# Strassen down projection of a float32 trunk: first sums on POOL, two more units split by ACT and DVE, two ACT steps moved

## The reference

```python
def conv_ffn(x, w_up, conv_w, conv_b, w_down):
    hdn = x @ w_up                                 # 512 x 1024 @ 1024 x 5632
    hdn = causal_dwconv(hdn, conv_w, conv_b)       # 3 taps along the tokens
    val, gate = jnp.split(hdn, [D_FF], axis=-1)    # D_FF = 2816
    return (jax.nn.gelu(gate) * val) @ w_down      # 512 x 2816 @ 2816 x 1024

...
for i in range(DEPTH):                             # DEPTH = 2
    ...
    ff = conv_ffn(x, f_w_up[i], f_conv_w[i], f_conv_b[i], f_w_down[i])
    x = layer_norm(ALPHA * x + ff, ln2_g[i], ln2_b[i])
    gate = jax.nn.sigmoid(x @ ple_gate_w[i] + ple_gate_b[i])
    x = x + gate * (p[i] @ ple_w[i])
```

## Time and profile before

| | before |
|---|---|
| median of three runs | 1246.64 us (1245.94 to 1247.58) |
| profiled execution | 1247.68 us, span 1245.6 us |
| PE busy | 1231.5 us (99%) |
| DVE busy | 731.9 us (59%) |
| ACT busy | 428.2 us (34%) |
| POOL busy | 731.8 us (59%) |
| granted clock, mean | 0.997 |

### The profile page before, as it was taken

The page is one execution under the profiler, slowest core; times in us unless marked ns, Lnnn a source line. Parts: engine busy times, 40 slices in busy tenths (PEclk is TensorE's granted clock), DMA queues, the critical chain, the costliest instruction groups (busy, mean ns, idle before and its releaser), DMA issues.

```text
span 1245.6 us, 17102 instructions
## 1 busy us (share of the span) xinstructions
PE 1231.5 (99%) x5733; PEld 1000.0 (80%) x5733; DVE 731.9 (59%) x1112; ACT 428.2 (34%) x719; POOL 731.8 (59%) x994
## 2 busy tenths in 40 slices
PE   9999999999999999999999999999999999999998
PEld 6887777788888888778788778888888888778787
DVE  6555556565545644898744374374644443898842
ACT  4445444222222123661244484112222222662141
POOL 7554467719877774005677547929887775003673
PEclk9999999999999999999999999999999999999999
DMA  5211132303322232864243212312222233675221
GB/s 198 70 68 68 68 118 89 115 8 111 101 101 97 89 132 70 262 197 150 85 170 102 82 71 85 119 52 102 101 101 93 92 101 118 203 220 168 85 93 60
DMA packets 74194, 137.44 MB, mean 110 GB/s; under 512 B 4272, under 2 KB 52976, under 8 KB 73632
## 3 DMA queue, kind: packets, MB, share of 16 engines
q1 hardware_dynamic: 73088, 134.23, 32.6%
q10 hardware_dynamic: 1056, 2.58, 0.6%
HBM read 134.60 MB, written 2.20 MB: 110 GB/s over the span
## 4 chain that ended last, share of the span: by engine, by line
PE 87%; DVE 4%; POOL 3%; POOLq 1%; DMA 1%; ACT 1%; issue 1%; DVEq 1%; ACTq 0%; SPq 0%
PE bank L540 19%; PE bank L542 19%; PE bank L541 19%; PE bank L559 3%; PE bank L561 3%; PE bank L560 3%; PE bank L834 2%; PE bank L836 2%; PE bank L841 2%; PE bank L896 2%; PE bank L898 2%; PE bank L897 2%; POOL w_lo L526 2%; DVE w_lo L1390 2%; PE bank L655 1%; POOLq L523 1%
## 5 line engine op out<-in xcount | busy, mean ns | idle before, releaser
L526 POOL TENSOR_TENSOR w_lo<-stage,w_hi 128x256 fp32r<-128x256 f32 x672 | 493.5, 765 | 24.8 <-issue 1.5
L520 POOL TENSOR_SCALAR w_hi<-stage 128x1024 fp32r<-128x1024 f32 x168 | 183.9, 1094 | 290.7 <-DVE w_lo L1390 179.1
L540 PE MATMUL bank<-x_hi,w_hi 128*128 128x512 f32 (+1 forms) x712 | 275.7, 387 | 0.0
L542 PE MATMUL bank<-x_hi,w_lo 128*128 128x512 f32 (+1 forms) x712 | 275.3, 387 | 0.0
L541 PE MATMUL bank<-x_lo,w_hi 128*128 128x512 f32 (+1 forms) x712 | 275.3, 387 | 0.0
L1292 DVE SCALAR_TENSOR_TENSOR tmp<-bank,cols,tmp 128x511 f32<-128x511 f32 x88 | 65.6, 745 | 204.7 <-ACT tmp L1735 204.7
L1735 ACT ACTIVATE tmp<-bank,cols 128x512 f32<-128x512 f32 x88 | 63.9, 778 | 294.5 <-PE bank L542 272.8
L542 PEld LDWEIGHTS bank<-x_hi,w_lo 128*128 128x128 f32 x712 | 133.7, 188 | 27.3
L541 PEld LDWEIGHTS bank<-x_lo,w_hi 128*128 128x128 f32 x712 | 133.7, 188 | 27.1
L540 PEld LDWEIGHTS bank<-x_hi,w_hi 128*128 128x128 f32 x712 | 133.7, 188 | 27.0
L540 PE MATMUL bank<-in_hi,w_hi 128*128 128x512 f32 x312 | 130.0, 417 | 0.0
(11 more groups left out here) (220 smaller groups left out, 2071.2 us busy)
## 6 DMA issues: line engine op xcount, KB each, us to landing
stage<-w_square SPq DMA_DIRECT2D x163, 512.0 KB, 3.2
stage<-w_down SPq DMA_DIRECT2D x56, 512.0 KB, 4.1
stage_far<-w_down SPq DMA_DIRECT2D x20, 512.0 KB, 4.4
rows<-norm_rows SPq DMA_DIRECT2D x4, 1024.0 KB, 5.7
outT<-x SPq DMA_DIRECT2D x7, 256.0 KB, 2.0
x<-xT SPq DMA_DIRECT2D x3, 512.0 KB, 6.8
p_in<-pT ACTq DMA_DIRECT2D x2, 512.0 KB, 4.8
w_ai<-w_lru SPq DMA_DIRECT2D x1, 1024.0 KB, 8.3
```

Source lines behind the costliest of these rows:

```text
L520: whole = pool.tensor_scalar(high[:, s, :], stage[:, s, :], 1.0, 0.0, ALU.mult, ALU.add)
L526: piece = pool.tensor_tensor(low[:, s, to], stage[:, s, to], high[:, s, to].bitcast(F32), ALU.subtract)
L540: pe.matmul(out, w_hi[:, s, c:c + P], m_hi, start=first, stop=False)
L542: return pe.matmul(out, w_lo[:, s, c:c + P], m_hi, start=False, stop=last)
```

## The change

DVE gives its first add of every step to POOL. In the first pass POOL's `first_sums` is the old add; in the second pass `near_sums` is the first of the three adds, and DVE's `second_sums` waits for it and makes the other two. Two of the six ordinary units, 32 and 33, are loaded, split and counted with the Strassen units (OWN = 34): ACT makes their high halves after the last Strassen unit, DVE the low half of 32 after that of unit 31, and that of 33 after eight of its folds. POOL splits 34 to 37. The split of these 34 units is counted on a semaphore of its own, `fold_low`; POOL adds 34 to `unit_split` ahead of its sums. The high half of the side of step 1 gets a place of its own, `second_hi`, over a part of `tmp`; ACT makes it, and the high half of unit 2, before the late convolution copies. ACT copies kept_b before the high half of unit 18.

```diff
+OWN = FOLD_UNITS + 2
...
+        second_hi = place("second_hi", [P, 3, SEQ // 2], F32R, [tmp_at])
...
             def down_loads(layer, ph):
-                for r in range(FOLD_UNITS):
+                for r in range(OWN):
                     last = fold_before(r)
...
                     elif last is not None:
-                        sp.wait_ge(unit_split, ph.done(0, last))
+                        sp.wait_ge(fold_low, layer * OWN + last + 1)
...
-                for r in range(FOLD_UNITS, len(ph.slots)):
-                    s, n = ph.slots[r], r - FOLD_UNITS
-                    last = [m for m in range(FOLD_UNITS) if fold_stage(m) == s][-1] if n < SLOTS else r - SLOTS
-                    sp.wait_ge(unit_split, ph.done(0, last))
+                for r in range(OWN, len(ph.slots)):
+                    s = ph.slots[r]
+                    last = [m for m in range(OWN) if fold_stage(m) == s][-1]
+                    sp.wait_ge(fold_low, layer * OWN + last + 1)
...
+            def first_sums(layer, i):
+
+                pool.wait_ge(fold_loaded[fold_stage(2 * i)], fold_fills(layer, 2 * i))
+                unit = pair_of(staged(2 * i))
+                pool.tensor_tensor(unit[:, :, 0, :], unit[:, :, 0, :], unit[:, :, 1, :], ALU.add)\
+                    .then_inc(first_summed, 1)
+
+            def near_sums(layer, i):
+
+                r = FOLD + 2 * i
+                for n in (r, r + 1):
+                    pool.wait_ge(fold_loaded[fold_stage(n)], fold_fills(layer, n))
+                far, near = pair_of(staged(r)), pair_of(staged(r + 1))
+                pool.tensor_tensor(near[:, :, 0, :], near[:, :, 0, :], far[:, :, 0, :], ALU.add)\
+                    .then_inc(near_summed, 1)
...
+                if ph.own:
+                    pool.drain()
+                    pool.sem_inc(unit_split, OWN)
+                    for i in range(PRE):
+                        first_sums(int(name[-1]), i)
+                    for i in range(PRE):
+                        near_sums(int(name[-1]), i)
...
-                        if ph.own and r == ph.own:
-                            pool.wait_ge(unit_split, ph.done(0, r - 1))
...
             def second_sums(layer, i):
...
-                for n in (r, r + 1):
-                    dve.wait_ge(fold_loaded[fold_stage(n)], fold_fills(layer, n))
+                dve.wait_ge(near_summed, layer * PRE + i + 1)
                 far, near = pair_of(staged(r)), pair_of(staged(r + 1))
-                dve.tensor_tensor(near[:, :, 0, :], near[:, :, 0, :], far[:, :, 0, :], ALU.add)
-                dve.drain()
...
             def fold_down(layer):
...
-                    if i + 1 < PRE:
-                        first_sums(layer, i + 1)
-                    else:
+                    if i + 1 == PRE:
                         second_sums(layer, 0)
...
+                unit_low(layer, FOLD_UNITS)
                 dve.wait_ge(product_done, layer * 3 + 2)
...
                     folded_in = block_fold(2 + tau, 0, banks[6 + tau], False, True)
                 folded_in.then_inc(bank_folded, 1)
+                unit_low(layer, FOLD_UNITS + 1)
                 dve.wait_ge(product_done, layer * 3 + 3)
...
                     unit_top(layer, 2 * i)
+                    if i == 1:
+                        conv_own(layer, last, 1)
                     unit_top(layer, 2 * i + 1)
-                    if i == 0:
-                        conv_own(layer, last, 1)
...
                         keep(6, kept_e)
+                        act.wait_ge(product_done, layer * 3 + 1)
+                        keep(4, kept_b)
                     unit_top(layer, FOLD + 2 * i)
                     if i == 1:
-                        act.wait_ge(product_done, layer * 3 + 1)
-                        keep(4, kept_b)
                         act.wait_ge(unit_used, ph.done(0, FOLD - 1))
                         keep(0, kept_d)
                     unit_top(layer, FOLD + 2 * i + 1)
+                unit_top(layer, FOLD_UNITS)
+                unit_top(layer, FOLD_UNITS + 1)
```

More of the change, by code:

```diff
@@ L139, in plan @@
     for name, slots, iters in want:
-        own = FOLD_UNITS if name.startswith("down") else 0
+        own = OWN if name.startswith("down") else 0
         last_used[SLOTS:] = [first - 1] * SLOTS
@@ L287, in hybrid_trunk_kernel @@
             sem(n) for n in ("fold_summed", "fold_high", "side_high", "side_ready"))
-        fold_sides_ready = sem("fold_sides_ready")
+        fold_sides_ready, first_summed, near_summed, fold_low = (
+            sem(n) for n in ("fold_sides_ready", "first_summed", "near_summed", "fold_low"))
         product_done, bank_kept, bank_folded, kept_read = (
@@ L367, in fold_fills @@
             s = fold_stage(r)
-            each = [fold_stage(n) for n in range(FOLD_UNITS)]
+            each = [fold_stage(n) for n in range(OWN)]
             return 16 * (layer * each.count(s) + each[:r + 1].count(s))
@@ L375, in side_slot @@
         def side_slot(step):
-            return step - 1 if step < PRE else step - 2
+            return step - 2 if step < PRE else step - 3
         def side_place(step):
@@ L388, in high_of @@
                 return first_hi[:, 0:3, :] if step < PRE else first_hi[:, 3:7, :]
+            if step == 1:
+                return second_hi[:]
             return side_hi[side_slot(step) % JIT][:, 0:3 if step < PRE else 4, :]
@@ L414, in down_unit, with rest_source @@
                 return w_down[u:u + 4, :, kp * 2 * P:(kp + 1) * 2 * P].rearrange("a p n -> p a n")
+            def rest_source(layer, r):
+                n = r - FOLD_UNITS
+                return down_unit(layer, n // (REST // 2), PRE + n % (REST // 2))
             def down_loads(layer, ph):
-                for r in range(FOLD_UNITS):
+                for r in range(OWN):
                     last = fold_before(r)
@@ L917, in fold_phase @@
                     first, last, step, r = i == 0, i == PRE - 1, PRE + i, FOLD + 2 * i
-                    unit_ready(ph, 0, r)
+                    fold_ready(layer, r)
                     pe.wait_ge(side_ready, layer * 2 * PRE + side_place(step))
@@ L929, in fold_phase @@
                         fold_product(layer, step, r, 1, 2, 6, False, last).then_inc(unit_used, 1)
-                    unit_ready(ph, 0, r + 1)
+                    fold_ready(layer, r + 1)
                     if first:
@@ L951, in down_phase @@
                 for k in range(REST):
-                    if k % 2 == 0:
+                    if k % 2 == 0 and FOLD_UNITS + k // 2 < OWN:
+                        fold_ready(layer, FOLD_UNITS + k // 2)
+                    elif k % 2 == 0:
                         unit_ready(ph, 0, FOLD_UNITS + k // 2)
@@ L1120, in summed @@
                 else:
-                    dve.wait_ge(unit_used, ph.done(0, ph.own + (half + 1) * (len(ph.slots) - ph.own) // 2 - 1))
+                    dve.wait_ge(unit_used, ph.done(0, len(ph.slots) // 2 * (half + 1) - 1 if n % 2 == 0 else
+                                                    FOLD_UNITS + REST // 2 * (half + 1) - 1))
                 bank = ln_bank(n, t, half)
@@ L1383, in unit_low @@
                 ph = phases[f"down{layer}"]
-                dve.wait_ge(fold_high, layer * FOLD_UNITS + r + 1)
+                dve.wait_ge(fold_high, layer * OWN + r + 1)
                 s = ph.slots[r] % SLOTS
@@ L1402, in fold_down @@
                 ph, last = phases[f"down{layer}"], FT // 2 - 1
-                first_sums(layer, 0)
-                dve.wait_ge(unit_split, phases[f"up{layer}"].done(last, 3))
                 for i in range(PRE):
@@ L1752, in side_top @@
                 ph = phases[f"down{layer}"]
-                if step % PRE:
-                    before = [n for n in range(step) if n % PRE and side_slot(n) == side_slot(step) - JIT]
+                if step % PRE and step > 1:
+                    before = [n for n in range(2, step) if n % PRE and side_slot(n) == side_slot(step) - JIT]
                     act.wait_ge(unit_used, ph.done(0, 2 * before[0] + 1) if before else
@@ L1767, in unit_top @@
                 ph = phases[f"down{layer}"]
-                if r >= FOLD:
-                    act.wait_ge(fold_summed, layer * 2 * PRE + PRE + (r - FOLD) // 2 + 1)
-                elif r % 2 == 0:
-                    act.wait_ge(fold_summed, layer * 2 * PRE + r // 2 + 1)
+                if FOLD <= r < FOLD_UNITS:
+                    act.wait_ge(fold_summed, layer * PRE + (r - FOLD) // 2 + 1)
+                elif r < FOLD and r % 2 == 0:
+                    act.wait_ge(first_summed, layer * PRE + r // 2 + 1)
                 else:
```

22 lines of the change are left out of this document (9 added, 13 removed).

## The result

| | before | after |
|---|---|---|
| median of twelve runs each | 1246.16 us (1244.36 to 1248.3) | 1248.9 us (1246.92 to 1250.39) |
| ratio after to before | | 1.0017 [1.0009, 1.0024] |
| span of the profiled execution | 1245.6 us | 1246.1 us |
| granted clock, mean | 0.997 | 0.999 |

The change costs 2.1 us (1.1 to 3.0), where 3.4 was forecast.

What follows compares the result with a forecast made beforehand. PE sets the time, with DVE almost fully busy and POOL free. Strassen part +0.8 and ordinary units +0.9 give 1.7 us a layer, 3.4 for both, on 1246.64: 1250.0 us; own range 1247.5 to 1253, range 1242.5 to 1254.5.

Steps and rivals of the forecast that it cites:

- The moves: ACT's high halves ahead of its convolution copies, kept_b ahead of unit 18; with DVE's relief they could give 2.65 us a layer.
- The price of a collision: A POOL add of 512 meeting a DVE operation with two SBUF inputs costs DVE 1.1 us, of 1.09 to 1.26.
- The third rival: Both passes: an add holds DVE for its whole length, 1.37 us a collision; a layer loses 4.4 us, 1255.4 us; chance 0.12.
- The first pass: DVE up to unit 11's low half: 1.8 us earlier start, -2.4 for four sums dropped, +3.3 for three of five collisions.
- The start of the second pass: Behind unit 11: unit 17's load 4.87 us, POOL's sum about 1.4; DVE's first remaining sum -0.3 us against 528.88.
- The sum: Whole kernel: 0.8 + 0.9 = 1.7 us a layer, 3.4 us for both layers, 1250.0 us.
- The ordinary units: After the Strassen part: unit 35's load waits behind unit 33's low half, so PE's wait for POOL grows by 0.9 us a layer.
- The rival of idle DVE: First-pass sums find DVE idle, fewer than about two of five collide; a layer gains 1.3 us, 1244.0 us; chance 0.18.
- nothing comes of it: Rival: with one or two collisions DVE's loss equals the moves' gain, tail unchanged, 1246.6 us; chance 0.22.
- The signs named beforehand: No first-pass ACT waits, POOL adds over 1.2 us, longer DVE operations, second-pass DVE waits, late unit 35 load, POOL wait 2 us or more.
- The rival that all waits go: If unit 35's load came early enough for POOL to end before PE, 6.45 us a layer are won: 1233.7 us; chance 0.05.

Runs made afterwards that it cites:

- the experiment on before: The kernel before with the two ACT moves alone (second_hi, and kept_b ahead of unit 18): ratio 0.9981 to before, 2.4 us under it.
- first sums on DVE: The changed kernel with only the first pass's sums back on DVE: ratio 1.0017 to before, 2.1 us over it.
- early loads: The changed kernel with units 34 to 37 loaded into the buffers of units 28 to 31, so no load waits for 32 or 33: ratio 0.9977 to before.
- the place of two pairs of transposes: All sums on DVE plus early loads, with two transpose pairs of the layer norm's output three steps later: 0.9920 to before, 3.1 us under the same without.
- the kernel with idle adds: The changed kernel with all sums on DVE and sixteen POOL adds a layer that nobody reads or waits for: ratio 1.0122 to before.

## Why the prediction was right in sign and a little too high

**The moves: right.** 2.65 us a layer were counted as won; alone they shorten the Strassen part by 2.1 and 2.7. That this need not reach the end was not in the text, and the experiment on before shows it.

**The price of a collision: right (1.1 taken, 1.11 measured), for a reason that the text half had.** The third rival's argument, that what a piece hides may be a fixed part of each instruction, is what the rows show (0.18 us of 0.73, of 1.04 and of 1.29). It did not come out at 1.37, because the add itself is short: 1.29 us, the lower end of the bounds. The reason that the text gave for taking the lower end, DVE's drain between its two remaining sums, is not what the rows show: all seven collisions lie on low halves and sides. That part of the size is luck.

**The first pass: right.** Three sums cost DVE 1.1 us each, in the first two rows below and at 519.40. Two low halves of 128x512 take 1.81 us when no sum lies there (523.11) and 2.92 when one does; the 128x512 h_raw takes 0.69 (at 494.19) and 1.79. The other two of the five cost 0.09 us and nothing:

```profile
505.48 2.92 DVE L1416 TENSOR_TENSOR w_lo<-stage,w_hi 128x512 fp32r<-128x512 f32 x2
...
516.82 1.79 DVE L1346 TENSOR_TENSOR h_raw<-tmp 128x512 f32<-128x512 f32 x1
...
523.11 1.81 DVE L1416 TENSOR_TENSOR w_lo<-stage_far,w_hi 128x512 fp32r<-128x512 f32 x2
```

The low half of unit 11 ends at 522.33, where the sum put it (523.15 - 1.8 - 2.4 + 3.3 = 522.25). The chain of work after the change, from that low half to DVE's first remaining sum:

```profile
519.48 2.85 DVE w_lo L1416 x2
522.33 0.02 issue
522.35 3.63 DMA stage<-w_down
525.98 0.02 issue
526.00 0.02 POOLq L525
526.02 0.10 issue
526.12 1.30 POOL stage L527
527.41 0.02 issue
527.44 0.69 DVE stage L1396
```

**The start of the second pass: the step that was off.** The sum had -0.3 us for DVE's first remaining sum, against 528.88. It came at 527.44, 1.44 early. The load of unit 17 took 3.63 us where 4.87 was carried over the earlier trace rows, and the add 1.30 where about 1.4 was taken. From there on the working holds: seven collisions at 1.1 less six adds are +3.1, measured 565.90 - 564.20 + 1.44 = 3.14. So the low half of unit 27 came at 565.9 in place of 567.0, and the Strassen part, +0.8 in the forecast, came out at -0.1 and -0.3 in this execution. A load's length differs between executions: this one took 4.98 us with the first sums on DVE and 4.90 with early loads. The kernel with early loads is the changed kernel up to the ordinary units, and with its 4.90 us the Strassen part of the first layer came out 1.0 over before (80.01), close to the forecast 0.8. Over the three kernels with the second-pass sums on POOL and the moves (after, first sums on DVE, early loads) the Strassen part is 79.26 us in the mean of both layers, 0.3 over before.

**The ordinary units: right (0.9 forecast, 1.1 to 1.2 measured: 36.71 + 1.6 - 37.22 in the first layer, with the low clock that it was spared counted in, and 38.44 - 37.21 in the second).** With the Strassen part ending at F = 579.70, unit 33 was split at F + 2.65 (forecast 2.5), unit 35 landed at F + 6.9 (6.3; 4.2 us where 3.8 was taken), and POOL needed 15.2 us for three units (15.6): unit 37 at F + 22.15, forecast 21.9. That the queue behind unit 33 is the cause is shown by the early loads: the wait for POOL goes.

**The sum.** (0.3 + 1.1) x 2 = 2.8 us, and by this execution alone (-0.2 + 1.1) x 2 = 1.8; the runs say 2.1, and some 2.7 at an equal count of low clocks (the estimate above). The forecast took the low clock as unchanged; that it came less often was not in it. The text also held that 2.5 us could not be told from no change: twelve runs of each told 2.1. The rival of idle DVE fell in the first pass (three collisions, not less than two), and at -0.1 to -0.3 the Strassen part shows none of its 2.2 us; that nothing comes of it is out by little, the interval of the ratio begins at 1.0009. The signs named beforehand all came: no wait for ACT, adds of 1.29 us, DVE operations of 1.14 from start to start that take two, three waits for low halves in the second pass, unit 35's load behind unit 33's low half. The rival that all waits go needed an early load, as the text said; given one, the waits did not all go, because DVE's layer norm stood next. Three figures of the text don't follow from its own rows, and little hangs on them: with no collision in the first pass the chain starts at -1.8 - 2.4 + 0.6 = -3.6 (it has -3.3), 3.3 us before 567.0 is 563.7 (564.0), and the lower bound of an add of 512 comes to about 2 x 0.73 - 0.22 = 1.24 (1.28).

## What to carry to other kernels

Before work goes from DVE to POOL, compare what DVE saves with what it loses each time the two meet: the row of POOL's instruction alone, less the little that overlaps. Where DVE is busy nearly throughout and its operations read two operands from SBUF, nearly every such move meets it, and an add that costs DVE 0.77 us is no bargain at 1.11. And take each gain past the next wait before counting it: here 2 us a layer stopped at POOL's last unit, and when that was freed, at the layer norm behind it; a load's place in its queue and the place of two pairs of transposes together (4.9 and 3.1 us) were worth more than taking all the sums back (4.1).

## What the runs showed that was not expected

The low clock does not follow each long wait of PE. The changed kernel's wait for unit 37 in the second layer:

```profile
1167.57 0.51 PE L590 MATMUL bank<-w_hi,h_hi 128*128 128x512 f32 x1 [2.28 <-POOL w_lo L557]
1167.91 0.49 PE L591 MATMUL bank<-w_lo,h_hi 128*128 128x512 f32 x1
1168.20 0.63 PE L592 MATMUL bank<-w_hi,h_lo 128*128 128x512 f32 x1
1168.63 0.63 PE L590 MATMUL bank<-w_hi,h_hi 128*128 128x512 f32 x1
```

Here the starts come 0.43 us apart, after the equal wait in the first layer (601.91, shown above) 0.24. In the seven profiles whose ordinary part has a wait of 1.9 to 2.3 us for POOL there are fourteen such waits; behind eight of them six to eight starts came 0.42 to 0.43 us apart (the 1.2 GHz level), behind six none did, with 2.28 or 2.29 us of idle time on both sides (both waits of 1.91 us before were followed by them). Behind waits of 1.4 to 1.6 us (the transposes above, and the kernel with idle adds) none did. A span with the low clock and one without differ by about 1.6 us for each, as much as this change was worth; what decides it stays open. In the four kernels with early loads, where the wait for POOL is gone, 19 of 24 runs have a mean clock of 1.0. So of the 2.9 us that early loads alone win over before, some 1.8 are the clock (an estimate: 0.2 low stretches a run against 1.3 in the runs of before on the same chip, at 1.65 us).
